# One expert layer on Trainium2: the gate table by adding DMAs in place of one-hot matmuls, 96 rows of U beside it, and a V stage of its own

## The reference, cut to what matters

```python
# 8 heads, 128 keys a side, 128*128 experts, top 16
s = jnp.einsum('phcd,hckd->phck', qy, sub_keys)
top_s, top_i = lax.top_k(s, PEER_TOPK)
cand_s = top_s[:, :, 0, :, None] + top_s[:, :, 1, None, :]
cand_i = top_i[:, :, 0, :, None] * N_KEYS + top_i[:, :, 1, None, :]
best_s, best_j = lax.top_k(cand_s.reshape(PEER_BLOCK, PEER_HEADS, PEER_TOPK * PEER_TOPK), PEER_TOPK)
experts = jnp.take_along_axis(cand_i.reshape(PEER_BLOCK, PEER_HEADS, PEER_TOPK * PEER_TOPK), best_j, axis=-1)
gate = jax.nn.softmax(best_s, axis=-1)
u = expert_u[experts]
v = expert_v[experts]
act = jax.nn.gelu(jnp.einsum('pd,phkd->phk', xb, u), approximate=False)
return jnp.einsum('phk,phkd->pd', (gate * act.astype(f32)).astype(xb.dtype), v)
```

## Time and profile before

| | |
|---|---|
| runs | 5230.61, 5233.93, 5234.56 us |
| span of the profiled execution | 5233.6 us (the page gives no other time of that execution) |
| TensorE busy | 4500.1 us, 86% of the span |
| DVE, ACT, POOL busy | 2581.1, 1306.9, 238.2 us |
| mean granted clock of TensorE | 0.908 |
| DMA | 466.09 MB, 89 GB/s over the span |

### The profile page before, as it was taken

One profiled execution on the slowest core, in us unless ns is written; L12 is line 12 of the kernel. 1 busy time (PEld: TensorE's weight loads), 2 busy tenths in 40 slices (PEclk: granted clock), 3 DMA queues, 4 the chain that ended last, 5 costly groups with the idle time before them and its releaser, 6 DMA issues. The chain is left out here.

```text
span 5233.6 us, 70974 instructions
## 1 busy us (share of the span) xinstructions
PE 4500.1 (86%) x22202; PEld 3776.3 (72%) x22202; DVE 2581.1 (49%) x6096; ACT 1306.9 (25%) x1861; POOL 238.2 (5%) x387
## 2 busy tenths in 40 slices
PE   6699755557668799888888799999999999999997
PEld 1699755556556677677777678888888888888886
DVE  1322265544356677666667544444444444444444
ACT  0200133332121122244444322222211211222220
POOL 0000011101000000000000000000000000000000
PEclk9799865668878899999999899999999999999998
DMA  5222100012211122245445532222222222222222
GB/s 210 98 94 91 61 23 22 22 46 91 90 39 32 44 78 80 72 105 140 125 128 139 135 114 96 96 96 91 85 93 88 92 81 96 96 96 96 96 96 89
DMA packets 416993, 466.09 MB, mean 89 GB/s; under 512 B 277138, under 2 KB 312162, under 8 KB 415842
## 3 DMA queue, kind: packets, MB, share of 16 engines
q1 hardware_dynamic: 365476, 285.48, 17.6%
q0 software_dynamic: 45056, 166.74, 10.0%
q10 hardware_dynamic: 6336, 12.58, 0.6%
HBM read 335.75 MB, written 129.00 MB: 89 GB/s over the span
## 5 line engine op out<-in xcount | busy, mean ns | idle before, releaser
L322 PE MATMUL evo<-vhi,Hhi 128*128 128x512 f32 x2048 | 800.9, 391 | 24.8 <-DVEq L51 24.8
L1589 DVE TENSOR_TENSOR acc<-acc,evo 128x512 f32<-128x512 f32 x512 | 352.0, 688 | 944.0 <-PE evo L324 934.0
L324 PE MATMUL evo<-vhi,Hlo 128*128 128x512 f32 x2048 | 797.8, 390 | 0.0
L323 PE MATMUL evo<-vlo,Hhi 128*128 128x512 f32 x2048 | 797.5, 389 | 0.0
L322 PEld LDWEIGHTS evo<-vhi,Hhi 128*128 128x128 f32 x2048 | 384.7, 188 | 117.2 <-issue 36.8
L324 PEld LDWEIGHTS evo<-vhi,Hlo 128*128 128x128 f32 x2048 | 384.7, 188 | 80.1
L323 PEld LDWEIGHTS evo<-vlo,Hhi 128*128 128x128 f32 x2048 | 384.9, 188 | 79.0
L1505 ACT ACTIVATE uhi<-etb 128x512 fp32r<-128x512 f32 x128 | 76.6, 598 | 1335.6 <-PE etb L1603 1318.5
L322 PE MATMUL epa<-h2hi,uhi 128*128 128x512 f32 x1024 | 404.8, 395 | 0.0
L324 PE MATMUL epa<-h2hi,ulo 128*128 128x512 f32 x1024 | 399.4, 390 | 0.0
L323 PE MATMUL epa<-h2lo,uhi 128*128 128x512 f32 x1024 | 398.7, 389 | 0.0
(11 more groups left out here) (277 smaller groups left out, 7639.7 us busy)
## 6 DMA issues: line engine op xcount, KB each, us to landing
gates_dram<-gstage SPq DMA_DIRECT2D x16, 4096.0 KB, 21.5
gr<-gates_dram POOLq DMA_DIRECT2D x128, 512.0 KB, 3.7
vraw<-in_expert_v SPq DMA_DIRECT2D x128, 512.0 KB, 5.1
ur<-in_expert_u SPq DMA_DIRECT2D x64, 512.0 KB, 3.4
ga<-ahead_dram POOLq DMA_DIRECT2D x64, 512.0 KB, 4.3
gwi<-in_w_in POOLq DMA_DIRECT2D x16, 1216.0 KB, 6.7
proj_dram<-gyi SPq DMA_DIRECT2D x128, 152.0 KB, 1.8
aurb<-in_expert_u POOLq DMA_DIRECT2D x32, 512.0 KB, 3.6
```

Source lines behind the costliest of these rows:

```text
L322: pe.matmul(out, lhi, rhi, start=(k == 0), stop=False)
L323: pe.matmul(out, lhi, rlo, start=False, stop=False)
L324: return pe.matmul(out, llo, rhi, start=False, stop=(k == n - 1))
L1589: link(dve.tensor_tensor(at, at, vo[u % 4][:, :], ALU.add), vo_add.sem)
```

## The change

`mixer_phase` fills the table `gates` with zeros: POOL clears one tile `blank` first, SP stores it 16 times behind each load of `prj`, 128 times 512 KB. `best_phase` no longer transposes; it computes the flat place of each slot, (i*128 + j)*1024 + token, as an integer, and keeps the weight as it is (slots along the row, tokens on partitions). Its loads of U go from POOL to SP and take rows 0 to 31. `gate_phase` is replaced by `scatter_phase`: POOL issues one indirect DMA for each slot of each tile, which adds 128 weights (one of each token) to 128 places of the table, and waits after each head until all its DMAs have landed; the 96 other rows of U run through `Ahead` on the other engines. `expert_phase` has only the V part left, with two sets of H and V tiles, 8 banks, and DVE's preparation of the next group spread over the first 12 units of the present one; SP issues all its loads. `ahead` grows to all 128 rows.

```diff
@@ mixer_phase, sync @@
+                sp.wait_ge(blank_done, 1)
                 with sp.Fori(0, TT // 2) as turn:
                     for p in range(2):
                         sp.wait_ge(tile_free.sem, tile_free.free(turn * 2 + p))
                         sp.dma_start(prj[:, p], proj[bass.ds((turn * 2 + p) * P, P), 0:W]).then_inc(prj_in[p], 16)
+                        for i in range(PER_TILE):
+                            at = (turn * 2 + p) * PER_TILE + i
+                            sp.dma_start(gates[bass.ds(at, 1)].rearrange("o j t -> (o j) t"), blank[:, :]).then_inc(blank_out, 16)
+                sp.wait_ge(blank_out, 16 * NKEYS)
...
@@ best_phase, sync @@
-                with sp.Fori(0, TT) as t:
+                def tile(t, last):
                     for j in range(R):
-                        A.store(sp, t * R + j, t * R + j)
+                        r = t * R + j
+                        if not (last and j >= R - 2):
+                            A.load(sp, r + 2, j % 2)
+                        A.store(sp, r)
...
@@ best_phase, vector @@
+                    link(dve.scalar_tensor_tensor(expert[:, :], pick[:, 0], float(NKEYS), pick[:, 1], ALU.mult, ALU.add))
+                    link(dve.tensor_scalar(IDX[:, bass.ds(t, 1)].rearrange("p o s -> p (o s)"), expert[:, :], float(T),
+                                           token[:, bass.ds(t, 1)], ALU.mult, ALU.add))
                     dve.wait_ge(be_done, t + 1)
                     link(dve.tensor_reduce(den[:, :], best[:, :, :], AX, ALU.add))
                     link(dve.reciprocal(den[:, :], den[:, :]))
-                    link(dve.tensor_tensor(pick[:, 2].rearrange("p (h k) -> p h k", h=HEADS), best[:, :, :],
-                                           den[:, :, None].to_broadcast([P, HEADS, TOPK]), ALU.mult), pick_done)
+                    link(dve.tensor_tensor(W[:, bass.ds(t, 1)].rearrange("p o (h k) -> p (o h) k", h=HEADS), best[:, :, :],
+                                           den[:, :, None].to_broadcast([P, HEADS, TOPK]), ALU.mult))
                     cut(3)
-                    dve.wait_ge(pick_mm, t + 1)
-                    for c, dst in enumerate((iT, jT, wT)):
-                        link(dve.tensor_copy(dst[:, bass.ds(t * P, P)], pt[:, c]), *[pick_cp] * (c == 2))
...
-def gate_phase(nc, iT, jT, wT, gates, h2hi, h2lo, expert_u, ahead, keep):
+def scatter_phase(nc, IDX, W, gates, h2hi, h2lo, expert_u, ahead, keep):
+    ROWS = NKEYS - ROWS_BEST
+        A = Ahead(nc, ctx, sem, K, h2hi, h2lo, expert_u, ahead, "s", ROWS_BEST, ROWS)
+        cells = gates.rearrange("i j t -> (i j t)")[:, None]
+        put = [sem(f"put{h}") for h in range(HEADS)]
...
+                for h in range(HEADS):
+                    if h:
+                        pool.wait_ge(put[h - 1], 16 * TT * TOPK)
+                    for t in range(TT):
+                        for k in range(TOPK):
+                            s = h * TOPK + k
+                            pool.indirect_dma_start(cells, bass.IndirectOffsetOnAxis(ap=IDX[:, t, s:s + 1], axis=0), W[:, t, s:s + 1], None,
+                                                    compute_op=ALU.add).then_inc(put[h], 16)
+                pool.wait_ge(put[HEADS - 1], 16 * TT * TOPK)
...
@@ scatter_phase, tensor @@
+                        if not (last and p):
+                            A.transpose(pe, r + 1, 1 - p, turn + p)
+                        for h in range(2):
+                            A.multiply(pe, r, p, h)
...
@@ expert_phase, sync @@
+                with sp.Fori(0, GROUPS // 2) as turn:
+                    for m in range(2 * Q):
+                        n = turn * (2 * Q) + m
+                        rows = bass.ds(n * P, P)
+                        sp.wait_ge(vlo_done.sem, vlo_done.free(n))
+                        sp.dma_start(vr[:, m % VS], expert_v[rows, :]).then_inc(v_in[m % VS], 16)
+                        sp.wait_ge(H_done.sem, H_done.free(n))
+                        sp.dma_start(ga[:, m % GS], ahead[bass.ds(n, 1)].rearrange("o e t -> (o e) t")).then_inc(a_in[m % GS], 16)
+                        sp.wait_ge(Hlo_done.sem, Hlo_done.free(n))
+                        sp.dma_start(gr[:, m % GS], gates[bass.ds(n, 1)].rearrange("o j t -> (o j) t")).then_inc(g_in[m % GS], 16)
...
@@ expert_phase, vector @@
+                def group(turn, p, last):
+                    g = turn * 2 + p
+                    ahead_turn, ahead_p = (turn, 1) if p == 0 else (turn + 1, 0)
                     for u in range(UNITS):
+                        q, step = divmod(u, 3)
+                        if q < Q and not last:
+                            (gate, cut_v, cut_H)[step](ahead_turn, ahead_p * Q + q)
                         dve.wait_ge(vo_mm.sem, vo_mm.done(g * UNITS + u))
+                        dve.wait_ge(vo_add.sem, vo_add.free(g * UNITS + u))
                         at = acc[:, u // 2, (u % 2) * HALF:(u % 2 + 1) * HALF]
-                        link(dve.tensor_tensor(at, at, vo[u % 4][:, :], ALU.add), vo_add.sem)
+                        dve.tensor_tensor(at, at, vo[u % BANKS][:, :], ALU.add).then_inc(vo_add.sem, 1)
...
-    ahead = dram("ahead_dram", [NKEYS // 2, NKEYS, T])
+    ahead = dram("ahead_dram", [NKEYS, NKEYS, T])
```

More of the change, by code:

```diff
@@ L1083, in __init__ @@
         self.tb, self.pa = ([ctx.enter_context(nc.psum_tensor(f"{n}{tag}{i}", [P, HALF], F32)) for i in range(2)] for n in ("atb", "apa"))
-        self.u_in = [one.start(rows // 2) for one in keep.soft[0:2]]
+        self.u_in = [sem(f"au_in{tag}{p}") for p in range(2)]
         self.ut_mm, self.uhi_done, self.ulo_done = (Steps(sem(n + tag), 2) for n in ("aut_mm", "auhi_done", "aulo_done"))
@@ new lines, in _, with body @@
+                pool.wait_ge(put[HEADS - 1], 16 * TT * TOPK)
+            @block.sync
+            def _(sp):
+                def body(turn, last):
+                    for p in range(2):
+                        r = turn * 2 + p
+                        if not last:
+                            A.load(sp, r + 2, p)
+                        A.store(sp, r)
+                A.load(sp, 0, 0)
+                A.load(sp, 1, 1)
+                turns(sp, body)
+                A.landed(sp)
+            @block.scalar
@@ L1420, in expert_phase @@
-def expert_phase(nc, h2hi, h2lo, expert_u, expert_v, gates, ahead, acc, keep):
+                    for p in range(2):
+                        r = turn * 2 + p
+                        if not (last and p):
+                            A.transpose(pe, r + 1, 1 - p, turn + p)
+                        for h in range(2):
+                            A.multiply(pe, r, p, h)
+                A.transpose(pe, 0, 0, 0)
+                turns(pe, body)
+def expert_phase(nc, expert_v, gates, ahead, acc, keep):
@@ L1474, in group @@
-                def group(g, last):
-                    for i, q in enumerate(ORDER):
-                        sp.wait_ge(vlo_done.sem, vlo_done.free(g * Q + i))
-                        sp.dma_start(vr[:, i % 2], expert_v[bass.ds(g * (Q * P) + q * P, P), :]).then_inc(v_in[i % 2], 16)
-                        if i % 2 and not last:
-                            load_u(g + 1, i // 2)
-                load_u(0, 0)
-                load_u(0, 1)
-                turns(sp, group)
-            @block.gpsimd
@@ L1591, in _ @@
-                link(dve.memset(acc[:, :, :], 0.0))
-                cut_u(0, 0)
-                turns(dve, group, link, 2 * 2 + Q * 5 + UNITS)
+                        dve.tensor_tensor(at, at, vo[u % BANKS][:, :], ALU.add).then_inc(vo_add.sem, 1)
+                dve.memset(acc[:, :, :], 0.0).then_inc(acc_clear, 1)
+                dve.wait_ge(acc_clear, 1)
+                for q in range(Q):
+                    gate(0, q)
+                    cut_v(0, q)
+                    cut_H(0, q)
+                turns(dve, group)
```

395 lines of the change are left out of this document (120 added, 275 removed).

## The result

The changed kernel takes 5628.89 us (median of 4 runs, 5627.41 to 5633.16) against 5232.27 of the kernel before in the same comparison (5225.94 to 5234.56): ratio 1.0759, 95% interval 1.0747 to 1.0772. It is 7.6% slower. Forecast was 4810 us, faster. The profiled execution took 5633.16 us, with a span of 5631.5 and a mean granted clock of 0.853.

The account below looks back on a forecast made before the run. TensorE's own instructions were taken to bound the last two stages. Scatter stage 1150 us for 800 (+350), V stage 1422 for 2196 (-774) and mixer +1, against a span of 5233.6, gave 4810 us, range 4780 to 5500.

Parts of the forecast that it names:

- the price x of one adding DMA: Scatter stage, POOL: 0.53 us for a plain DMA plus two passes of 0.23, 1.0 in all; 1048 us, hidden by 92.
- the bounds: Scatter stage: an adding DMA costs between 0.53 us (plain POOL DMA) and 2.0 us (each must land before the next).
- the likeliest case: Scatter stage: adding DMAs hidden behind TensorE's rows of U while one costs under 1.09 us; 4810 us, chance 0.40.
- a sign of being wrong: Between last U and first V product: POOL issuing, TensorE still, as long as the excess of 1024x over 1116 us.
- C: Scatter stage: each adding DMA finishes before the next, by completion or descriptor loop; decides from 1.50 us; 5742 us, chance 0.28.
- B: Scatter stage: POOL bounds but change still pays; runs built one by one, 1.25 us a DMA; 4975 us, chance 0.27.
- The figure of the Trainium skill: Scatter stage: about 2.0 us fixed per POOL DMA plus its bytes; end to end the sum would be 5742 us.
- The V stage: After the scatter stage: starts at 3354, fill 28 us, 512 units at 2.72 are 1393, last product at 4776.
- Double buffering: V stage: two sets of tiles by themselves save only TensorE's 24.8 us of waits before the V products.
- The zeros in the mixer: Mixer: stores of 67 MB, 43 us a tile, hidden in a tile's 64.9 us, but for 1 us on the first load.
- the pick: Best stage: removing the picks wins nothing at a tile's end; the next row's cut ends the 6.1 us wait.
- Rival D: Scatter stage: small adds crowd the 16 DMA engines, loads of U land late, TensorE waits each row; 5216 us, chance 0.05.

## Why the prediction was wrong

**The step that failed** is the price x of one adding DMA: "I take the nearest row, 0.53, and two small POOL passes over 128 partitions for offsets and addresses (0.23 each, as the iota): 1.0". It is 1.86 from start to start, 1.91 on the mean. Two terms were too small and two were missing. The passes were priced by a POOL instruction that fills a tile; a list of places costs 0.43 (0.96 against 0.53) and adding 0.34 (0.87 against 0.53), not 0.23 each. Both together cost 1.02 of busy time, 0.25 more than the two alone, and the gap of 0.30 stands before each one with a list; neither was in the sum. With the measured 1.86 the prediction's own arithmetic gives 4810 + 1024 x 1.86 + 24 - 1140 = 5599 us, 30 under the result; the rest is in the longer gaps now and then and in a first DMA at 2217 in place of 2210.6. 1.86 lies between the bounds, 0.53 and 2.0, but the upper one by luck: it was to be the price if each DMA had to land before the next, and landing takes 3.0. The range was cut at x = 1.76, though the nearest row had neither a list nor an addition, and the likeliest case was put 0.09 us from its own breaking point, 1.09. What it named as a sign of being wrong, a stretch with POOL issuing and TensorE still, is what came.

**Which rival it was.** C gave the sign, and its point of decision, x = 1.50, is borne out: 1.91 is over it. Its mechanism, that each is read, added and written back before the next is taken, fell in the form of completion: the next is issued 1.86 us on while the one before takes 3.0 us to land, and the DMA engines are busy 0.22 of the time. Its other form, a descriptor loop, is B's mechanism at a higher price. What the runs show is nearer to B's, at a price that B did not reach (1.25): POOL is the bound, and pays both for the addition and for the list, with 1.55 us of its own busy time. But it is no bill by the run, as B pictured it: a number costs 2.3 ns, the DMA 1.26 us at each size tried. What POOL does in these 1.26 us, and in the gap of 0.30, no view shows. The Trainium skill (Perfetto Trace Analysis, "DMA Instruction — SWDGE (GPSIMD)") says that the profiler's end of such an instruction is where the last processor of GpSimd has written its last descriptor, and not where the data has landed. The trace agrees: 1.55 us of instruction, 3.0 to landing.

**The figure of the Trainium skill** (DMA: Bandwidth & Descriptors), 2.0 us for each such DMA, taken end to end, gave 5742. That is 2% over the result, by luck. The forecast set it aside since plain loads are issued 0.70 us apart, and for plain DMAs the trace was right (0.53 in the run of direct ones). That page of the Trainium skill puts its figure on completion, and completion isn't what is paid here: 1.86 us is POOL's issuing, and the landing, 3.0 us after the issue, doesn't hold up the next one.

**What held.** First product for U at 2223.2 (forecast 2218.6), the last one at 3353.9 (3347.5): 96 rows in 1130.7 us, 11.8 each as before. The V stage: fill 25.4 us from the first load to the first product (28), then 1393.9 (1393) with no wait at all. Double buffering was to buy 24.8 us; the run with all tiles by matmuls is 14 faster in all, which would fit a fill 11 us longer than the old 14, but that difference was not taken apart. The zeros in the mixer: forecast hidden but for 1 us; the last tile starts 6 us later, of which 3 were there at the first. That is within the noise: the best stage's first transpose starts anywhere from 1771.2 to 1786.7 in the runs with zeros, and at 1778.6 in the one trace before. (The prediction's price of zeros at half rate was worked out wrong, without effect: 8.4 MB at 97 GB/s take 86 us a tile and not 81, so 169 in all and not 130.) The best stage: the end of a tile in the changed kernel, two rows of TensorE's timeline,

```profile
2103.13 0.39 PE L324 MATMUL apab<-h2hi,aulob 128*128 128x512 f32 x1
...
2109.32 0.78 PE L322 MATMUL apab<-h2hi,auhib 128*128 128x512 f32 x1
```

is 6.2 us long, and 6.3 with the pick in it: it did not set the wait, and taking it out bought nothing, as forecast. The stage as a whole even takes 4 us more, which the forecast had at nothing: 428.9 from the first transpose to the last product (1781.2 to 2210.1), and 424.8 before (1778.6 to 2203.4). Rival D was not seen here (loads of U land in 3.8 us), but in the two runs with direct DMAs.

## What to carry to other kernels

Before many small DMAs replace a computation, find how many there are and divide the time that they may take by it; if the answer is near the price of the nearest DMA in the trace, and that one has no list of places and no addition, the forecast isn't "hidden" but "measure one". Here an adding DMA of 128 numbers cost POOL 1.86 us, alone on the core or not, and an eighth as many numbers saved 14% of it. Where a cheap engine takes over work that an expensive one did, share it out until both end together: six tiles of eight, and one of them issued in a stage where POOL was idle, turned a loss of 7.6% into a gain of 5.6%.

## What was not expected of the hardware

Plain indirect writes issued back to back by POOL all but stop the rest of the core: 143 matmuls in 400 us where 1901 ran beside adding DMAs, one TensorE instruction for each POOL instruction, at 128 numbers and at 16 alike. The adding form of the same DMA, 0.6 us longer on POOL, holds up no other engine, and direct plain ones, with their places side by side, delay only the loads of U (142 us in all). Why the addition frees the other engines stays open.
